# Gate and up projections of a float32 trunk layer by 2x2 block products in seven multiplications, two of four weight sums made by accumulating DMA

## The reference, cut to what matters

```python
D_FF = ((8 * D_MODEL // 3 + 255) // 256) * 256        # 2816 = 22 x 128

def swiglu(x, wg, wu, wd):
    return (jax.nn.silu(x @ wg) * (x @ wu)) @ wd

x = x + 0.5 * swiglu(rms_norm(x, g_ffn1), w_ffn1_gate, w_ffn1_up, w_ffn1_down)
y, st = hybrid_mixer(rms_norm(x, g_mix), ...)         # projection of 1024 x 4104, two recurrences, output projection
x = x + y
x = x + 0.5 * swiglu(rms_norm(x, g_ffn2), w_ffn2_gate, w_ffn2_up, w_ffn2_down)
```

## Time and profile before

| | us |
|---|---|
| median of 3 runs | 1133.25 |
| lowest and highest | 1133.13 to 1133.56 |
| the profiled execution's own time | 1132.77 |
| its span in the trace | 1131.0 |
| PE busy in the span | 1113.8 |
| DVE busy | 504.5 |
| ACT busy | 327.3 |
| POOL busy | 219.8 |

### The profile page before, as it was taken

One profiled execution on the slowest core, in us unless ns is written; L12 is line 12 of the kernel. 1 busy time (PEld: TensorE's weight loads), 2 busy tenths in 40 slices (PEclk: granted clock), 3 DMA queues, 4 the chain that ended last, 5 costly groups with the idle time before them and its releaser, 6 DMA issues.

```text
span 1131.0 us, 21336 instructions
## 1 busy us (share of the span) xinstructions
PE 1113.8 (98%) x8860; PEld 1110.0 (98%) x8860; DVE 504.5 (45%) x710; ACT 327.3 (29%) x457; POOL 219.8 (19%) x182
## 2 busy tenths in 40 slices
PE   7999999999999999999999999999999999999997
PEld 7999999999999998999999999999999999999997
DVE  6433333333343355564655556543333433424333
ACT  7222222222222134333322224422222222212212
POOL 2221221222100020021232322222212222200000
PEclk9999999999999998999999999999999999999999
DMA  7333233232322376847486224532332332133222
GB/s 211 94 93 91 76 93 93 75 88 66 101 81 75 88 120 93 71 64 73 73 66 77 68 74 57 141 99 79 91 93 78 89 93 81 55 103 89 65 75 80
DMA packets 186845, 98.14 MB, mean 87 GB/s; under 512 B 6208, under 2 KB 185448, under 8 KB 186664
## 3 DMA queue, kind: packets, MB, share of 16 engines
q1 hardware_dynamic: 186792, 97.37, 38.5%
HBM read 94.07 MB, written 3.28 MB: 86 GB/s over the span
## 4 chain that ended last, share of the span: by engine, by line
PE 96%; DVE 1%; ACT 1%; issue 0%; DMA 0%; SPq 0%; POOL 0%; ACTq 0%
PE dense L456 89%; PE dense L558 1%; PE core_banks L644 1%; PE core_banks L659 1%; PE core_banks L662 1%; PE core_banks L634 1%; PE core_banks L456 1%; DMA x_tok<-in_x_prompt 0%; DVE rstd L1026 0%; PE core_banks L671 0%; PE core_banks L628 0%; PE core_banks L630 0%; PE core_banks L545 0%; PE core_banks L492 0%; PE core_banks L695 0%
## 5 line engine op out<-in xcount | busy, mean ns | idle before, releaser
L456 PE MATMUL dense<-xg_hi,w_hi 128*128 128x272 f32 x1920 | 402.2, 291 | 1.7 <-DVE xg_lo L1020 1.7
L456 PE MATMUL dense<-xg_lo,w_hi 128*128 128x272 f32 x1920 | 396.8, 288 | 0.0
L456 PE MATMUL dense<-xg_hi,w_lo 128*128 128x272 f32 x1920 | 396.4, 287 | 0.0
L1015 DVE TENSOR_TENSOR w_lo<-w_raw,w_hi 128x1024 fp32r<-128x1024 f32 (+2 forms) x191 | 254.9, 1341 | 255.5 <-ACT w_hi L784 255.0
L456 PEld LDWEIGHTS dense<-xg_lo,w_hi 128*128 128x128 f32 x1920 | 303.3, 189 | 0.0
L456 PEld LDWEIGHTS dense<-xg_hi,w_hi 128*128 128x128 f32 x1920 | 300.2, 188 | 2.3 <-issue 1.9
L456 PEld LDWEIGHTS dense<-xg_hi,w_lo 128*128 128x128 f32 x1920 | 300.4, 188 | 0.0
L784 ACT ACTIVATE w_hi<-w_raw 128x1024 fp32r<-128x1024 f32 (+1 forms) x192 | 182.3, 959 | 82.1 <-PE dense L456 80.0
L456 PE MATMUL dense<-h_hi,w_hi 128*128 128x272 f32 x660 | 137.4, 290 | 0.0
L456 PE MATMUL dense<-h_lo,w_hi 128*128 128x272 f32 x660 | 136.1, 287 | 0.0
L456 PE MATMUL dense<-h_hi,w_lo 128*128 128x272 f32 x660 | 136.0, 287 | 0.0
(11 more groups left out here) (238 smaller groups left out, 741.6 us busy)
## 6 DMA issues: line engine op xcount, KB each, us to landing
w_raw<-in_w_ffn_gate SPq DMA_DIRECT2D x44, 512.0 KB, 3.9
w_raw<-in_w_ffn_up SPq DMA_DIRECT2D x44, 512.0 KB, 3.8
w_raw<-in_w_in SPq DMA_DIRECT2D x32, 512.0 KB, 8.3
w_raw<-in_w_ffn_down SPq DMA_DIRECT2D x32, 384.0 KB, 3.3
w_raw<-in_w_ffn_down SPq DMA_DIRECT2D x32, 320.0 KB, 3.3
w_raw<-in_w_out SPq DMA_DIRECT2D x8, 512.0 KB, 3.7
out<-y_tok SPq DMA_DIRECT2D x4, 512.0 KB
x_tok<-in_x_prompt SPq DMA_DIRECT2D x3, 512.0 KB, 4.9
```

The lines of the kernel that those rows point to most:

```text
L456: last = nc.tensor.matmul(out[:, half, 0:TH], w[:, s % 4, k, :], x(kt)[:, half * TH:(half + 1) * TH], start=start and n == 0 and m == 0, s ...
L1015: nc.vector.tensor_tensor(w_lo[:, s % 4, 0:nk, :], w_raw[:, s % RAW, 0:nk, :], w_hi[:, s % 4, 0:nk, :].bitcast(F32), ALU.subtract).then_in ...
```

## The change

In each feed-forward stage the first 4 of 22 column tiles of gate and of up stay as they are (8 plain units). The other 18 tiles are taken two at a time, a pair of gate tiles (even p) and then the same two up tiles (odd p), 18 pairs per stage and 36 in all. For a pair, x is seen as 2x2 blocks (frame halves of 272 by k halves of 4 tiles) and the weights as 2x2 blocks (k halves by column tile). The four result blocks come from seven products instead of eight, each of 4 k-tiles and three passes, 12 matmuls of 272 columns.

Each product needs an x operand, of which four are sums of x blocks and three are blocks, made once per stage from x times gain times rstd (`x_hat`, `x_sum`, then `x_op_hi` and `x_op_lo`), and a weight operand, of which three are blocks and four are sums of blocks. Two of the four weight sums (operands 1 and 4) are made by a DMA that POOL issues and that adds a second block of the weights in HBM to a block already loaded in SBUF; the other two (2 and 6) are made on DVE. The products are accumulated in three banks in the order 0, 1, 0, 2, 0, 1, 0; ACT copies products 0, 1, 2 and 4 out as they end (`kept`), and DVE combines them. Weight operands of odd pairs are loaded into `w_raw`, of even pairs into a new buffer `w_src`. There is one slot for each of the seven operands in `w_hi` and `w_lo`, freed by its product of the pair before.

Since the new buffers take room, h has 12 tiles instead of 22 and the down projection is done in two chunks, over 12 and over 10 tiles, each added to the residual. POOL no longer makes `gate_r` and `h_lo` for the pairs. All loops are written out. The diff, cut to its core:

```diff
+    STD = 4
+    PAIRS = (range(0, 8), range(8, 18))
+    FC, F0 = (12, FT - 12), (0, 12)
+    DOWN_K = [[(0, 6), (6, 12)], [(0, 5), (5, FT - 12)]]
+    BLOCKS = 7
+    BANK = (0, 1, 0, 2, 0, 1, 0)
+    OPENS = (0, 1, 3)
+    KEPT = (0, 1, 2, 4)
...
+            def load_pair(n, p, w):                               # SP
+                blocks = ((0, quarter(0, 0)), (1, quarter(0, 1)), (3, quarter(1, 0)), (4, quarter(0, 1)), (5, quarter(1, 1)))
+                for o, view in blocks:
+                    if p - 2 in PAIRS[p >= PAIRS[1][0]]:
+                        sp.wait_ge(block_lo, BLOCKS * (P_ - 2) + o + 1)
...
+                    sp.dma_start(source(e, o), view).then_inc(block_loaded[e][o], 16)
...
+            def add_blocks(n, p, w):                              # POOL
+                pool.wait_ge(block_loaded[e][1], 16 * (P_ // 2 + 1))
+                nc.gpsimd.dma_start(source(e, 1), quarter(0, 0), accum_op=ALU.add).then_inc(block_summed[e][1], 16)
+                pool.wait_ge(block_loaded[e][4], 16 * (P_ // 2 + 1))
+                nc.gpsimd.dma_start(source(e, 4), quarter(1, 1), accum_op=ALU.add).then_inc(block_summed[e][4], 16)
...
+            def pair(n, c, p):                                    # PE
+                for o in range(BLOCKS):
...
+                    if o == 2:
+                        pe.wait_ge(product_copied, 4 * P_ + 1)
+                    if o == 4:
+                        pe.wait_ge(product_copied, 4 * P_ + 3)
+                    if o == 6:
+                        pe.wait_ge(product_copied, 4 * P_ + 4)
+                    if p == 0:
+                        pe.wait_ge(x_op_ready, BLOCKS * n + o + 1)
+                    pe.wait_ge(block_lo, BLOCKS * P_ + o + 1)
+                    for k in range(KH):
+                        for m, (w, x) in enumerate(((hi, x_hi), (hi, x_lo), (lo, x_hi))):
+                            last = nc.tensor.matmul(banks[BANK[o]], w[:, k, :], x[:, k, :], start=o in OPENS and k == 0 and m == 0,
+                                                    stop=k == KH - 1 and m == 2, skip_group_check=o not in OPENS)
+                    last.then_inc(product_done, 1)
...
+            def pair(n, c, p):                                    # ACT
+                for o in range(BLOCKS):
+                    if o in KEPT:
+                        copy_product(n, p, o)
+                    next_hi(n, c, p, o)
+                    if e == 0 and p - 2 in PAIRS[c]:
+                        if o == 3:
+                            pair_h_to_hi(c, p - 2, Q - 1, 1)
+                        if o == 5:
+                            pair_h_to_hi(c, p - 2, Q - 1, 0)
+                    if e == 0 and o == 6:
+                        silu_first(Q)
+                    if e == 1 and o == 3:
+                        silu_second(Q)
+                    if e == 1 and o == 5:
+                        silu_last(n, p - 1, Q)
...
+            def sum_t2(n, p):                                     # DVE, waits for operand 1's accumulating DMA
+                nc.vector.tensor_tensor(source(e, 2), source(e, 1), source(e, 5), ALU.add).then_inc(pair_summed, 1)
...
+            def pair(n, c, p):                                    # DVE
+                for o in range(BLOCKS):
+                    if o == 0:
+                        if e == 0 and p - 2 in PAIRS[c]:
+                            up_last(n, p - 1, Q - 1)
+                        if more:
+                            sum_t2(n, p + 1)
+                    if o == 3 and more:
+                        sum_t4(n, p + 1)
...
+                    next_lo(n, c, p, o)
...
+            def plain(n, norm):                                   # DVE; ACT has its own with x_to_hi and block_to_hi
+                for u in range(2 * STD):
+                    if u + 2 < 2 * STD:
+                        split_lo(0, s + 2, 0)
+                    if u == 1:
+                        for k in range(3):
+                            make_x_hat(n, norm, k)
+                    if u == 2:
+                        for k in range(3, 6):
+                            make_x_hat(n, norm, k)
+                    if u == 3:
+                        make_x_hat(n, norm, 6)
+                        make_x_hat(n, norm, 7)
+                        make_x_sum(n, 0)
+                    if u == 4:
+                        make_x_sum(n, 1)
+                        make_x_sum(n, 2)
+                    if u == 5:
+                        sum_t2(n, 0)
+                        x_to_lo(n, 0)
+                    if u == 6:
+                        make_x_sum(n, 3)
+                    if u >= 5:
+                        block_to_lo(n, 0, 2 * (u - 5))
+                        if u == 6:
+                            sum_t4(n, 0)
+                        block_to_lo(n, 0, 2 * (u - 5) + 1)
+                    if u >= 6:
+                        x_to_lo(n, u - 5)
...
+            def first_pair(n):                                    # ACT during pair 0
+                copy_product(n, 0, 0)
+                block_to_hi(n, 0, BLOCKS - 1)
+                x_to_hi(n, 4)
+                copy_product(n, 0, 1)
+                x_to_hi(n, 5)
+                copy_product(n, 0, 2)
+                x_to_hi(n, 6)
+                block_to_hi(n, 1, 0)
+                block_to_hi(n, 1, 1)
+                block_to_hi(n, 1, 2)
+                copy_product(n, 0, 4)
```

More of the change, by code:

```diff
@@ L69, in hybrid_trunk_step @@
     U_F2 = U_OUT + DT
-    U_D2 = U_F2 + 2 * FT
-    U_END = U_D2 + 4 * DT
+    U_END = U_F2 + UNITS_F
+    U_STD = (U_F1, U_F2)
+    U_DOWN = [[u + 2 * STD + 2 * DT * c for c in range(2)] for u in U_STD]
     X_ORDER = (0, 1, NC, 2, 3)
@@ new lines, in ffn @@
+            def ffn(n, norm):
+                plain(n, norm)
+                for c in range(2):
+                    for p in PAIRS[c]:
+                        pair(n, c, p)
+                    down(n, c)
+            def plain(n, norm):
+                for u in range(2 * STD):
+                    s, t = U_STD[n] + u, T_STD[n] + u
+                    pe.wait_ge(w_lo_ready, s + 1)
+                    tile_free(t)
+                    if u == 0:
+                        product(s, bank_of(t), *xg, range(SUMS_K[norm]), True, False, ready=xg_ready(norm))
+                        if n:
+                            pe.wait_ge(y_ready, 2 * H)
+                        norm_sums_of(norm)
+                        product(s, bank_of(t), *xg, range(SUMS_K[norm], DT), False, True, ready=xg_ready(norm))\
+                            .then_inc(unit_done, 1)
+                    else:
+                        product(s, bank_of(t), *xg, range(DT), True, True).then_inc(unit_done, 1)
@@ L550, in last_tile @@
                 for part, cols in enumerate(LAST_COLS):
-                    for u, (a, b) in enumerate(DOWN_K):
+                    for u, (a, b) in enumerate(DOWN_K[1]):
                         if part == 0:
@@ new lines, in ffn @@
+            def ffn(n, norm):
+                plain(n, norm)
+                for c in range(2):
+                    if c == 0:
+                        first_pair(n)
+                    else:
+                        block_to_hi(n, PAIRS[1][0], BLOCKS - 1)
+                    for p in PAIRS[c][1:] if c == 0 else PAIRS[c]:
+                        pair(n, c, p)
+                    Q = pair_index(n, PAIRS[c][-1]) // 2
+                    pair_h_to_hi(c, PAIRS[c][-1], Q, 1)
+                    pair_h_to_hi(c, PAIRS[c][-1], Q, 0)
+                    down(n, c)
@@ new lines, in down @@
+            def down(n, c):
+                for j in range(DT):
+                    for u in range(2):
+                        k = 2 * j + u
+                        if c == 1 or k + 2 < 2 * DT:
+                            split_hi(0, U_DOWN[n][c] + k + 2, 0)
+                        if c == 0 and k >= 2 * DT - 3:
+                            o = 2 * (k - (2 * DT - 3))
+                            block_to_hi(n, PAIRS[1][0], o)
+                            block_to_hi(n, PAIRS[1][0], o + 1)
+                    if c == 0:
+                        continue
+                    if n and j == DT - 1:
+                        for part in range(2):
+                            last_part(part)
+                        return
+                    if n == 0:
+                        normed_hi(0, j, T_DOWN[n][c] + j, G_MIX, 0)
+                    else:
+                        act.wait_ge(evicted, T_DOWN[n][c] + j + 1)
+                        if j >= 2:
+                            act.wait_ge(out_turned, j - 1)
+                        act.wait_ge(gains_ready, 1)
+                        nc.scalar.activation(x_gain[:, j % 2, :], xT[:, j, :], ACT.Copy,
+                                             scale=gains[:, G_FINAL + j:G_FINAL + j + 1]).then_inc(x_gained, 1)
@@ new lines, in ffn @@
+            def ffn(n, norm):
+                plain(n, norm)
+                for c in range(2):
+                    if c == 0:
```

(11 more changed lines are left out.)

612 lines of the change are left out of this document (434 added, 178 removed).

## The result

| | before | after |
|---|---|---|
| median of the runs, us | 1133.34 (4 runs beside it) | 1087.7 (4 runs) |
| lowest and highest | 1133.13 to 1133.56 | 1085.02 to 1088.38 |
| the profiled execution / its span | 1132.77 / 1131.0 | 1087.44 / 1085.7 |

The ratio is 0.9593, 95% interval 0.9576 to 0.9609: 45.6 us less, against 45 forecast. First the page, for the earlier trace rows; its queue lines follow in the same fence.

What follows compares the result with a forecast made beforehand. The prediction took PE to bound the feed-forward stages at 125.6 ns per matmul. From 1132.77 us it took 54.2 for matmuls removed and added 8 for fill and 1 for boundaries: 1087.6, stated as 1088 us, range 1082 to 1116.

Steps and rivals of the forecast that it cites:

- Matmuls removed: Gate/up pairs: 84 matmuls instead of 96, 432 fewer over 36 pairs at 125.6 ns each, -54.2 us.
- Boundaries: Waits where one product follows another, 252 products instead of 72 units: +1 us, bounds 0 and 5.
- DVE, hidden: DVE's work in a double pair: 18.1 us against PE's 21.1, cost 0 on the path.
- Rival A: DVE becomes the bound in the pairs, two-input work slowed by 1.28: +27, 1115 us; chance 0.12.
- ACT and the copy, hidden: ACT in a double pair: 15.0 of 21.1 us, copies ending 0.5 to 0.7 us after their product, cost 0.
- The rule on PSUM banks: Skill's advice to rotate PSUM banks; bank 0 recurs every second turn, yet the copy has 0.8 us to spare.
- DMAs, hidden: Loads and accumulates of a pair: 8.3 us of DMA time within 10.55, cost 0.
- The factor 2: POOL's accumulating DMAs: a reducing DMA is half as fast as a copy, so twice the plain packet time.
- Rival B: Accumulating DMAs bound the pairs, slower than before from 11.8 us per pair; 1173 us at 130 ns; chance 0.14.
- Fill: Filling the pipe before and in each stage's first pair: 4.2 plus 3.8 us, +8 together, bounds 2 and 20.
- The walk: Step-by-step timing of stage 1's fill, evictions and first pair: PE waits 1.2, 2.2, 0.6 and 0.2, 4.2 us.
- Transitions and tail: Changes between pairs and down units, and the last tile's final sums: 0 to 0.4 us, taken 0.

Runs made afterwards that it cites:

- e8_order2: The reordered kernel with more ACT copies and splits and DVE low halves of x moved ahead of the last plain eviction: 1082.79 us.
- e2_dve_sums: Changed kernel with all four weight sums made on DVE and no DMA issued by POOL: 1091.3 us, ratio 0.9632.
- e10_short26: Changed kernel with products 2 and 6 of every pair cut to 3 matmuls each: 1022.89 us.
- e5_short: Changed kernel with product 5 of every pair cut to 3 of its 12 matmuls: 1059.47 us.
- the reordered kernel: Changed kernel with only ACT's and DVE's queue order changed around each stage's first pair, product 0 copied earlier: 1082.06 us, 1081.66 when run again.
- e4_eight: Changed kernel with product 5's twelve matmuls issued twice, so 96 per pair again: 1140.57 us, ratio to before 1.0067.
- e6_extra2: Changed kernel with four more accumulating DMAs of 256 KB per pair in each stage's second group of pairs: 1126.94 us.
- e7_extra1: Changed kernel with two more accumulating DMAs of 256 KB per pair in each stage's second group of pairs: 1086.39 us.

## Why the prediction was right, point by point

- **Matmuls removed, -54.2.** Right: 125.4 ns in the pairs against 125.6, and putting 12 per pair back costs 52.9 us. **Boundaries, +1**: nothing is seen, the chain runs on at 125.4 ns over them.
- **DVE, hidden.** Right in its effect. The term was too large: 18.1 us summed, 16.5 worked, because the durations of successive operations overlap. Rival A's factor 1.28 did not show in the pairs: low halves there take 0.68 or 0.69 us beside POOL's DMA issues. Single ones beside POOL's elementwise work in the fill took 1.7 (e8_order2). e2_dve_sums put 2.2 us more on DVE and e10_short26 took 3.6 us of cover away, and DVE did not become the bound.
- **ACT and the copy, hidden.** Right: a copy ends 0.43 us after its product inside the pairs. ACT's own term was too large as well, 15.0 us per double pair against 13.4. What I had not listed is the second deadline in ACT's queue, the last Silu of the gate pair, which has only 0.5 us to spare. It is the nearest bound behind PE.
- **The rule on PSUM banks** (the Trainium skill, Perfetto Trace Analysis, Matmuls). This trace agrees with the rows rather than with the worry: bank 0 every second product cost nothing at 12 matmuls per product, and cost PE 0.37 us per pair as soon as the product between had 3 (e5_short).
- **DMAs, hidden.** Right: 8.3 us per pair forecast, 9.1 measured. The five loads are 4.6 us as forecast (e2_dve_sums); two accumulates are 4.3 instead of 3.7.
- **The factor 2** (the Trainium skill, Collectives: The Full Stack, Part 3, bandwidth ceiling). The trace agrees nearly: 2.2 times a copy's engine time for the same bytes.
- **Rival B**, accumulates that hold PE, shows only with four more per pair, and the threshold of the forecast was wrong. It was put at 11.8 us of packet time per pair, where the saving would be used up; with 13.8 us nothing was lost. A limit of one accumulate per 2.5 us fits the two runs, where it sits is open. The change has more room here than the forecast gave it.
- **Fill, +8.** Measured 4.9 + 2.8 = 7.7, against 4.2 + 3.8. The walk held to 0.5 us up to eviction 4 (ends forecast at 32.4, 38.5, 45.2 and 51.8, found at 32.87, 38.80, 45.37 and 51.62). The part that failed is how the 4.2 us of stage 1 are made up: eviction 5 made PE wait 0.2 us instead of 1.2, the copy of product 0 cost 2.8 instead of 2.2, the waits of 0.6 and 0.2 behind it did not come, and 1.8 us came from a fall of the clock that no step had. The total is right partly by compensation, and that part of it is luck.
- **Transitions and tail, 0.** Between pairs and down units the chain goes on without a gap, and the mixer's time is the same to 0.04 us. The tail was mis-sized: 0.7 us longer, where the forecast had 0 to 0.4 and took 0. Boundaries (+1 forecast, 0 seen) make up for it.

## What to carry to other kernels

When an edit takes matmuls out of a PE-bound stretch, price them at the pitch of the chain; then list, for every bank that is reused, the operation that frees it and where it stands in its engine's queue, since here two such deadlines of 1.5 us (a copy and a Silu), not the 63% of DVE, are what the next saving runs into. The remaining loss is in the first pair of a stage: put copies that free PSUM ahead of a wait for another engine (5.6 to 6.0 us for an edit of the order alone, 4.6 of them in the two stages by the profiles), and stop when the engine behind is without gaps, as the second reordering shows. The best version seen is the reordered kernel at 1081.7 to 1082.1 us.

## What the runs showed of the hardware that was not expected

- The same wait of 2.8 us before product 2 of stage 1 was followed by the lower granted clock in 8 of the 10 profiled executions that have it, and not in two (e4_eight, e5_short). In stage 2 the wait of 2.3 us brought no fall in the changed kernel and four others, but did in e4_eight, e5_short, e6_extra2 and e10_short26; e2_dve_sums waits 2.8 us there, without a fall. Waits of 0.6 to 1.2 us in the reordered kernels brought none. Whether a wait of this length costs its own time or some 1.8 us more is not set by the wait alone.
- An accumulating DMA of 256 KB goes out as 528 packets, a plain copy from the same queue as 80. An accumulate took 2.13 us of each engine's time against 0.95 (queue shares of 14.1% and 6.3%), and landed after 5.6 us against 3.7; POOL was busy 1.28 us with each issue against 0.75.
- The DMA share of a window was 1.31 without any loss (e7_extra1) and 1.31 with a loss of 4.6 us per pair (e6_extra2). Reaching 1 is no sign of a bound.
